# Mixture-of-experts layer on one core: order within expert pairs, per-expert release of the up matrices, order of the routing lists

## The reference, cut to what matters

```
idx, wts = route(h, w_router, e_bias)          # 8 of 64 experts for each of the 384 tokens
y = (silu(h @ ws1) * (h @ ws3)) @ ws2          # the shared expert, all tokens
  + sum over the 8 chosen experts e of  wts * ((silu(h @ w1[e]) * (h @ w3[e])) @ w2[e])
x = LN2(alpha * x + gate2 * y)
```

## Time and profile before

| | us |
|---|---|
| median of three runs | 1279.81 |
| the profiled execution, its own time | 1282.54 |
| its span, first to last instruction | 1280.4 |
| TensorE busy in it | 1021.1 (80%) |
| DMA packets of SP's queue, share of 16 engines' time | 65.9% |

### The profile page before, as it was taken

How to read it: one execution, slowest core, us unless ns; L and a number is a source line. 1 busy time by engine, 2 the same in 40 slices (tenths; PEclk the granted TensorE clock), 3 DMA queues, 4 the chain that set the end, 5 groups by cost and what they waited for, 6 DMA issues and landing times.

```text
span 1280.4 us, 23838 instructions
## 1 busy us (share of the span) xinstructions
PE 1021.1 (80%) x8392; PEld 652.9 (51%) x8393; DVE 432.4 (34%) x835; ACT 276.5 (22%) x515; POOL 220.1 (17%) x364
## 2 busy tenths in 40 slices
PE   4899999977676999985768888887777778776665
PEld 3898878756565444543335554444344334433332
DVE  4433343447742313876312112111111111112118
ACT  2322223325464000111112222111111111111100
POOL 0011100001300000202223323232222222223101
PEclk9899999988898999997889999999998899899888
DMA  9575535547266195085995698999999999999865
GB/s 348 180 254 196 181 125 183 177 167 258 79 235 211 63 345 175 33 346 164 317 333 212 245 346 298 384 383 394 385 385 384 376 370 374 379 383 382 348 243 214
DMA packets 97896, 347.52 MB, mean 271 GB/s; under 512 B 15041, under 2 KB 20209, under 8 KB 73130
## 3 DMA queue, kind: packets, MB, share of 16 engines
q1 hardware_dynamic: 81162, 311.56, 65.9%
q0 software_dynamic: 13936, 30.13, 7.2%
q10 hardware_dynamic: 2736, 4.98, 1.1%
HBM read 329.41 MB, written 29.52 MB: 280 GB/s over the span
## 4 chain that ended last, share of the span: by engine, by line
DMA 24%; PE 21%; issue 4%; DVE 2%; SPq 1%; ACT 1%; DVEq 0%; POOLq 0%; POOL 0%; ACTq 0%
DMA W<-w 22%; PE PS L1914 8%; PE PS L1899 6%; PE PS L1930 3%; PE PS L1968 2%; PE PS L1954 2%; DMA hT<-h_rows,tokens 1%; PE PS L1888 1%; DVE hido L2030 1%; SPq L1439 1%; ACT sgo L1997 1%; PE PS L1922 0%; DVE hidTo L2033 0%; SPq L1440 0%; DMA W<-expert_rows 0%
## 5 line engine op out<-in xcount | busy, mean ns | idle before, releaser
L1899 PE MATMUL PS<-W,XT 128*32 128x256 f32 x2048 | 141.1, 435 | 65.6 <-DMA W<-w 57.0
L1899 PEld LDWEIGHTS PS<-W,XT 128*32 128x32 f32 x2048 | 83.9, 125 | 136.9 <-issue 115.4
L1914 PE MATMUL PS<-W,XTo 128*64 128x256 f32 x1216 | 139.4, 381 | 0.0
L1914 PEld LDWEIGHTS PS<-W,XTo 128*64 128x64 f32 x1216 | 88.9, 137 | 41.3 <-issue 4.6
L303 PE MATMUL PS<-w_hi,u_hi 128*128 128x512 f32 x240 | 94.2, 392 | 1.5 <-DVE w_lo L427 1.0
L303 PE MATMUL PS<-w_hi,u_lo 128*128 128x512 f32 x240 | 93.5, 389 | 0.0
L303 PE MATMUL PS<-w_lo,u_hi 128*128 128x512 f32 x240 | 93.4, 389 | 0.0
L1954 PE MATMUL PS<-middle,hidT 128*32 128x512 f32 x512 | 66.7, 625 | 31.8 <-issue 30.5
L427 DVE TENSOR_TENSOR w_lo<-raw,w_hi 128x2048 fp32r<-128x2048 f32 x26 | 59.5, 2288 | 89.4 <-ACT w_hi L369 89.4
L1983 ACT ACTIVATE sg<-PS 64x256 f32<-64x256 f32 x32 | 12.1, 378 | 355.1 <-PE PS L1899 355.1
L1930 PE MATMUL PS<-middle,hidTo 128*64 128x512 f32 x304 | 73.6, 601 | 16.3 <-DVE hidTo L2033 16.3
(11 more groups left out here) (375 smaller groups left out, 1537.6 us busy)
## 6 DMA issues: line engine op xcount, KB each, us to landing
W<-w SPq DMA_DIRECT2D x128, 1024.0 KB, 14.1
middle<-w SPq DMA_DIRECT2D x64, 1024.0 KB, 16.9
raw<-w_in SPq DMA_DIRECT2D x26, 1024.0 KB, 5.3
wada<-w_ada SPq DMA_DIRECT2D x6, 2048.0 KB, 7.6
W<-expert_rows SPq DMA_DIRECT2D x16, 512.0 KB, 9.7
kc<-cache_k_diff SPq DMA_DIRECT2D x8, 512.0 KB, 5.0
vc<-cache_v_diff SPq DMA_DIRECT2D x8, 512.0 KB, 3.7
middle<-expert_rows SPq DMA_DIRECT2D x8, 512.0 KB, 15.4
```

What stands on the lines that cost most here:

```text
L1899: mm = pe.matmul(PS[64 * h + 32 * c:64 * h + 32 * c + 32, UP_B + i, 0:F], XT[:, i, k, 32 * c:32 * c + 32], t.W13[:, 2 * i + c, h, k], star ...
L1914: mm = pe.matmul(PS[64 * h:64 * h + 64, XH_B, 0:F], XTo[:, k], t.W13[:, slot, h, k], start=k == 0, stop=k == KD - 1)
```

## The change

Three edits. (1) In `rank_i` the two progressions swap places: of a pair the expert with few tokens now stands first, the one with many second. (2) SP asks for the up matrices of pair n+2 expert by expert: after the pair's `up` and the extra blocks of the first place, the first two matrices; after the extra blocks of the second place, the other two. `load_up` and `load_down` take one slot instead of a pair for that. (3) In the routing TensorE does the list products of tiles 0 and 1 ahead of `shared_down` of tile 2.

```diff
-            pool.iota(both[:, :, 0], pattern=[[1, (E - WB) // 2]], base=WB, channel_multiplier=0).then_inc(iota_done, 1)
-            pool.iota(both[:, :, 1], pattern=[[-1, (E - WB) // 2]], base=E - 1, channel_multiplier=0).then_inc(iota_done, 1)
+            pool.iota(both[:, :, 1], pattern=[[1, (E - WB) // 2]], base=WB, channel_multiplier=0).then_inc(iota_done, 1)
+            pool.iota(both[:, :, 0], pattern=[[-1, (E - WB) // 2]], base=E - 1, channel_multiplier=0).then_inc(iota_done, 1)
...
+def load_up(sp, t, slot, e):
+
+    sp.dma_start(t.W13[:, slot, 0], of_expert(t.w1v, e)).then_inc(t.wup_in[slot // 2], 16)
+    sp.dma_start(t.W13[:, slot, 1], of_expert(t.w3v, e)).then_inc(t.wup_in[slot // 2], 16)
...
             pe.wait_ge(ws2_in, 16)
-            for n in range(NT):
+            for n in range(NT - 1):
                 shared_down(n)
-            for n in range(NT):
+            for n in range(NT - 1):
                 lists(n)
+            shared_down(NT - 1)
+            lists(NT - 1)
...
                     sp.wait_ge(h_mm, n + 1)
-                    used = sp.value_load(t.ov[0:1, bass.ds(n * 2 + 2, 1)], min_val=0, max_val=XB)
-                    sp.wait_ge(o_h, used + 1)
-                    stand_alone(sp)
-                    load_up(sp, t, i, of_next)
+                    for c in range(2):
+                        used = sp.value_load(t.ov[0:1, bass.ds(n * 2 + (c + 1), 1)], min_val=0, max_val=XB)
+                        sp.wait_ge(o_h, used + 1)
+                        stand_alone(sp)
+                        load_up(sp, t, 2 * i + c, of_next[c])
                     sp.wait_ge(yy_mm, n + 1)
                     stand_alone(sp)
-                    load_down(sp, t, i, of_next)
+                    for c in range(2):
+                        load_down(sp, t, 2 * i + c, of_next[c])
```

More of the change, by code:

```diff
@@ L1433, in of_expert, with load_down @@
     return w[e] if isinstance(e, int) else w[bass.ds(e, 1)].rearrange("e p k n -> (e p) k n")
[L1436 to L1446, removed]
+def load_up(sp, t, slot, e):
+    sp.dma_start(t.W13[:, slot, 0], of_expert(t.w1v, e)).then_inc(t.wup_in[slot // 2], 16)
+    sp.dma_start(t.W13[:, slot, 1], of_expert(t.w3v, e)).then_inc(t.wup_in[slot // 2], 16)
+def load_down(sp, t, slot, e):
+    sp.dma_start(t.W2[:, slot], of_expert(t.w2v, e)).then_inc(t.wdown_in[slot // 2], 16)
 def fetch_rows(pool, t, dst, places, done):
@@ L1504, in _ @@
             for i in range(PW):
-                first = [E // WB * (2 * i + c) for c in range(2)]
-                load_up(sp, t, i, first)
-                load_down(sp, t, i, first)
+                for slot in (2 * i, 2 * i + 1):
+                    load_up(sp, t, slot, E // WB * slot)
+                for slot in (2 * i, 2 * i + 1):
+                    load_down(sp, t, slot, E // WB * slot)
         @block.tensor
```

## The result

The changed kernel took 1269.88 us (median of 9 runs), the kernel before 1277.86 beside it on the same chip: ratio 0.9929, 95% interval 0.9902 to 0.9957. By the ratio that is 9 us less (5.5 to 12.5), where I forecast 4.0. One of the nine executions took 5505 us; it counts in the median and not in the ratio. The profiled execution took 1265.68 us (span 1263.6).

A forecast was written before the change was run, and what follows sets the result against it. TensorE was taken to pace the kernel up to pair 11, the weight transfers afterwards. Head start -5.3, pair 0 +0.5 and routing +0.8 gave -4.0 us: from 1279.8 to 1275.8 us, forecast range 1273.5 to 1278.5.

The forecast's parts named there:

- The routing: Term for the reordered lists: tile 2's list ends later, delaying the expert stage by 0.8 us, or 1.6 with a wait.
- The head start: Expert stage: light half of pair 9's up matrices goes out 10.9 us earlier, so the weight stream ends 5.3 us sooner.
- stall by row traffic: Rival, pairs 3 to 7: extra blocks' gathers and scatters share engines with the light half; one 7 us stall, 1282.8, chance 0.12.
- binding releases: Rival, late pairs: the 27.53 us is latency, not queue; 5.3 us saved in some nine steps, 1232, chance 0.03.
- evened engines: Rival: the swap moves busy rows and extra blocks' rows to different DMA engines, 6 us more come free, 1270, chance 0.09.
- From 794.97 on it never is [empty]: Weight stream: from SP's request for pair 9's up matrices the DMA queue is never empty until the last pairs.
- only makes the queue longer: Saturated stretch, from 970 us on: engines are never free, so an earlier release there gains nothing.
- My term of +0.5 for pair 0: Pair 0: an early load beside a late gather may delay its rows; 0.5 us lost, between 0 and 5.4.

The follow-up runs named there:

- e5: Only the third part of the change (list products of tiles 0 and 1 ahead of tile 2's shared product), against the kernel before: ratio 1.0017 (0.9987 to 1.0047).
- e2: Only the swap of the places, up matrices still released together, lists as before, against the kernel before: ratio 0.9990 (0.9965 to 1.0016).
- e7: Places swapped, lists as before; light half early only from pair 10 on, both halves together in pairs 0 to 9; against the kernel before: 0.9964.
- e11: The whole change, unchanged, measured a second time, against the kernel before: ratio 0.9918 (0.9890 to 0.9947).
- e3: Early release of the light expert's half without the swap, lists as before, against the kernel before: ratio 0.9929 (0.9904 to 0.9953).
- e4: The change without its third part (swap and release expert by expert, lists as before), against the kernel before: ratio 0.9921 (0.9892 to 0.9949).
- e12: The change without its third part, measured again beside the whole change on one chip; against the kernel before: ratio 0.9914 (0.9882 to 0.9946).
- e8: The change without its third part, light half also waiting until DVE has formed the pair's hidden rows; against the kernel before: 0.9907 (0.9872 to 0.9942).
- e1: The kernel before, unchanged, run again for a second profile: 1286.1 us (one run).
- e6: Places swapped, lists as before; light half early only in pairs 0 to 9, both halves together from pair 10 on; against the kernel before: 0.9923.
- e9: Places swapped, lists as before; both halves asked for together, only when the pair's last extra block is copied out; against the kernel before: 1.0003.
- e10: Places swapped, lists as before; first place's half at the old time, second's when the last extra block is copied out; against the kernel before: 0.9982.
- e13: Places swapped, lists as before; from pair 10 on both halves only when the last extra block is copied out; against the kernel before: 0.9973.
- e14: Places swapped, lists as before; from pair 10 on up matrices asked for only with the down matrices, after the down product; against the kernel before: 0.9957.
- e15: Places swapped, light half early everywhere; from pair 10 on busy half only when the last extra block is copied out; against the kernel before: 0.9888.
- e16: Places swapped, light half early everywhere; from pair 10 on busy half only after the pair's down product; against the kernel before: 0.9893.

## Why the prediction was wrong

**What held.** The routing: forecast 0.8 us later, measured 0.70 (e5 and the change). The head start: forecast 5.3; pairs 3 to 12 took 198.5 us before and 194.1 after, 4.4 less. Every kernel that is early up to pair 9 has H 193.1 to 194.6, every one that is pairwise there 197.2 to 199.1. No stall by row traffic came up, and nothing like the 48 us of binding releases. The rival that gave a time near the result, 1270 by evened engines, was wrong in its mechanism: e2 has the swap and no gain. The Trainium skill, "DMA: Bandwidth & Descriptors", section "The descriptor swizzle", gives the formula by which I took the swap to change nothing. It gives it for a transfer to 128 partitions, and I assumed it for gathers of 64 rows; e2's 0.9990 agrees.

**What failed** is the step "From 794.97 on it never is [empty]", with the sentence that an earlier release there "only makes the queue longer". By it the pace of the saturated stretch stays as it is, and the sum has no term for it. e7 shows the contrary: its light half is early from pair 10 on alone, and S is 324.7 us, against 328.8 to 330.3 in the four kernels that are pairwise throughout; its whole time is 0.9964 (0.9939 to 0.9989) of before. I read the step from shares of 1.01 and 1.02 over 16 and 36 us. A finer view of the same trace speaks otherwise. Before, 1 us at a time, around SP's request of 991.42 to 992.85 us:

```profile
989.00:990.00 1.00, 1.00 (x13) 0.66 (x10) 0.00 (x0) 0.00 (x0) 0.98 (x2) 1.00 0.89 369
990.00:991.00 1.00, 1.00 (x12) 0.49 (x8) 0.00 (x0) 0.00 (x0) 0.00 (x0) 1.00 0.96 352
991.00:992.00 1.00, 0.80 (x10) 0.57 (x8) 0.38 (x1) 0.54 (x2) 0.00 (x0) 1.00 0.74 193
992.00:993.00 1.00, 0.30 (x2) 0.20 (x2) 0.51 (x2) 1.00 (x2) 0.00 (x0) 1.00 1.05 311
```

After the change, around the requests at 1011.82 and 1015.31:

```profile
1010.00:1011.00 1.00, 1.00 (x20) 0.51 (x13) 0.00 (x0) 0.05 (x1) 0.00 (x0) 1.00 1.02 426
1011.00:1012.00 1.00, 1.00 (x14) 0.79 (x13) 0.55 (x1) 0.84 (x2) 0.18 (x1) 1.00 1.04 434
1012.00:1013.00 1.00, 1.00 (x14) 0.64 (x11) 0.07 (x1) 0.07 (x1) 0.32 (x1) 1.00 1.03 418
1013.00:1014.00 1.00, 1.00 (x12) 0.66 (x10) 0.00 (x0) 0.00 (x0) 0.87 (x2) 1.00 0.96 377
1014.00:1015.00 1.00, 1.00 (x11) 0.45 (x7) 0.00 (x0) 0.00 (x0) 0.00 (x0) 1.00 1.01 401
```

Before, a quarter of the engines' time is missing in the microsecond in which the request goes out, and the bytes fall to half (the view counts a packet where it starts). Counted packet by packet, 16 are under way up to 989.2 us, 12 from 991.25 to 992.25, and 16 again from 992.75, when the new loads move. The Trainium skill, "Perfetto Trace Analysis", section "Identifying the Most-Contended Engine", calls the occupancy of 16 DMA engines misleading; the trace agrees, 0.74 in one microsecond inside a stretch (920 to 1000 us) that reads 1.01. The share of the 16 engines in the 4 us around each request, from 954 us on in both (after: the light halves), is

```
before  0.97 1.04 0.93 1.05 0.91 1.03 0.86 1.05 0.79 1.04 0.94
after   1.00 1.01 1.02 1.02 1.02 0.95 1.02 0.87 1.01 0.95 1.01
```

Every second request of before finds engines run dry, down to 0.79 at 1104 us. After the change it begins later and is weaker (0.95, 0.87 and 0.95 at 1049, 1086 and 1121 us). It is so in the other profiles: counted as packets under way, the first such request from pair 8 on is that of pair 16 in all four pairwise kernels, and that of pair 19 to 22 in the seven with the change's releases in the stretch (after, e11, e3, e4, e12, e8, e7). A load is counted in 16 parts, and they don't land in step: the last 16 counts of U(31) come between 1207.1 and 1215.3 us, and its last two loads were full 9 us apart. I had that row, but drew nothing from it for the releases. Where 12 packets are under way ahead of a request and 16 behind it, some engines had nothing to do until SP asked again, however much the others still held.

How much is it? I counted the weight packets of the traces (8 KB each, 128 a matrix, 768 a pair). The lead is what had been moved when a pair's up product starts beyond what that pair needs (up matrices to its own, down matrices of earlier pairs), in matrices. The rate, the mean length and the share of time with fewer than 16 packets of any kind under way are those of S:

```
                      pair 0-3    H      S   lead at 12, 30  packets/us  ns   under 16
before                   69.2   198.5  330.3   1.9   3.4        42.5     339    6.1%
e1, before again         69.3   199.1  329.1   1.7   3.3        42.6     338    6.0%
e2, swap alone           69.3   198.2  328.8   1.8   3.2        42.6     340    4.9%
e5, lists alone          70.2   198.4  328.8   1.6   3.3        42.7     338    4.9%
after                    65.6   194.1  324.4   1.9   3.7        43.3     335    2.3%
e11, after again         68.0   193.4  324.5   2.0   3.6        43.2     336    2.3%
e3, early, no swap       69.1   194.6  323.1   2.1   3.6        43.4     334    3.1%
e4, lists as before      67.3   194.0  324.5   1.9   3.5        43.2     335    2.9%
e12, the same            69.3   193.2  324.8   1.8   3.7        43.3     335    2.4%
e8, light 0.4 later      67.0   193.9  324.4   1.6   3.3        43.3     335    2.5%
e6, early to 9           66.5   194.1  326.8   2.1   3.1        42.7     338    4.6%
e7, early from 10        71.0   197.8  324.7   1.4   3.7        43.5     335    2.2%
e9, late                 68.9   204.2  327.0   1.8   2.0        42.4     337    7.9%
e10, late split          68.4   197.7  328.9   1.5   3.2        42.7     338    5.1%
e13, late from 10        70.2   197.2  325.5   1.4   1.9        42.7     337    7.0%
e14, later from 10       69.2   197.8  324.7   1.6   1.7        42.6     336    6.8%
e15, busy half late      69.0   193.1  322.9   1.8   3.0        43.3     335    2.8%
e16, busy half later     67.7   193.9  325.5   1.7   3.2        43.0     335    4.9%
```

S is (18 x 768 + 128 x growth of the lead) / rate. That holds by the way the terms are counted and is no cause, but it parts S in two. *The rate:* with an early half from pair 10 on it is 43.0 to 43.5 in nine profiles, without it 42.4 to 42.7 in nine others. 1.5% of 329 us is 4.9 us, the missing gain. It comes about where the pairwise requests begin to find engines dry: from pair 12 to 18 the seven early kernels take 109.2 to 111.8 us and the four pairwise ones 110.0 to 111.3, from pair 18 to 30 they take 212.6 to 214.9 against 217.5 to 220.1. *The lead:* with pairwise requests 1.4 to 1.7 matrices more are moved ahead of need by pair 30; 1.5 are 192 packets, 4.5 us of all engines' work. With late requests (e9, e13, e14) it grows by 0.1 to 0.5 only, and S is 2.3 to 4.5 us shorter than the pairwise mean of 329.3, without any gain in rate. So asking earlier inside a saturated stretch isn't neutral, as I took it to be, nor is it good in itself: an early light half goes with a higher rate, a late request with a smaller lead. Whether the two add is open: with the busy half put off S is 322.9 in e15 and 325.5 in e16, against 324.4 for the change.

Summed for the change, against the pairwise kernels: routing +0.7; pairs 0 to 3, mean of the two profiles 66.8 against 69.5, -2.7; H -4.8; S -4.8; and pair 31 gives back some 1.1 us (16.3 us from pair 30 to 31, against 14.8 to 16.2). In all -10.5, beside the measured 9 and 10.5. The sum forecast +0.8, +0.5, -5.3 and nothing for these stages: the saturated stretch is the term that was left out, and pairs 0 to 3 came out the other way, for which no run gives the cause. The forecast's range of 1273.5 to 1278.5 doesn't follow from the bounds of its terms either, which add to 1274.2 at best (-5.5, 0, +0.8, -0.9) and 1282.8 at worst (-4.9, +5.4, +1.6, +0.9).

**What stays open.** *Why the rate is higher.* The rate is the weight packets under way divided by their length. From the four pairwise kernels to the seven with the change's releases the first goes from 14.43 to 14.51 (0.6% more) and the second from 338.7 to 334.8 ns (1.2% less). So engines kept from running dry are about a third of the gain in rate, and shorter packets two thirds. Of the weight packets that start in the 2 us after a pairwise request 15 to 17% take over 420 ns, after an early light half 0 to 2%; in all of S it is 11 to 12% and 10%. That may be engines that start from standstill; but the pairwise request also falls into the microseconds in which gathered rows arrive, when packets are long in every kernel (below), and the two aren't told apart. And e13 and e14 run dry still more often (7%) at an unchanged rate, with packets of 336 to 337 ns, while e16 with 4.9% has a rate of 43.0, so dry time alone isn't the measure. No trace names the engine that moved a packet. *Why moving ahead costs the others time:* that engines share something is the plain reading, but only argued. *Pairs 0 to 3:* the kernels that are early there take 65.6 to 69.3 us, the pairwise ones 69.2 to 71.0. Part of it is pair 1's 1.6 us, which is there in all early kernels but e15 and which no row explains. The rest may be the granted clock, which from 600 to 668 us changes between 2.4 and 1.2 GHz (a mean of 0.83 to 0.90 over the 18 profiles): pair 0's up product alone took 5.2 to 6.3 us, where 3.66 is usual. My term of +0.5 for pair 0 doesn't show: its wait for rows was 0.6 to 2.3 us in the early kernels and 0.8 to 2.4 in the pairwise ones.

## What to carry to other kernels

A mean busy share of 1.00 over several transfers doesn't say that an earlier request is worthless: look at it microsecond by microsecond around each request, and at the time between the last two counts of one load, before costing a deeper queue at nothing. Then ask for whom the earlier transfer is: here the half that was asked for early in the saturated stretch was worth 4.6 us there (e7), while asking late for what nobody yet needed was worth nearly as much (3.8 and 4.5 us, e13 and e14). And split a forecast into head start and pace, since a release that is moved in every pass of a loop acts on both. Last, read from the trace of an experiment whether its edit moved what it was to move: e8's wait looked like half of the lead and took off a tenth.

## What was unexpected of the hardware

The share of DMA time goes above 1 because packets overlap: from 900 to 1160 us of before, 17 packets were under way on the 16 engines for 19% of the time and 18 for 3%. So a share of 1.01 doesn't tell whether the engines are full: it is read from 803 to 819 us, where there were never fewer than 16 packets, and from 920 to 1000 us, where there were fewer for 5% of the time.

A weight packet takes 314 ns as a rule, but 394 to 508 ns (means of single microseconds) from 991 to 997 us of before, where rows of 4 KB arrive. POOL had issued a gather at 988.79 and one at 994.23, and no scatter until 997.07, so these are gathered rows; beside the row packets from 1002 to 1005, behind scatters of 997.07 and 999.78, weight packets take 310 to 316. It is so in all 18 profiles: in the stretch from 2.5 to 0.5 us ahead of a gather's landing weight packets take 384 to 456 ns, ahead of a scatter's 310 to 315.

And asking 4.7 to 6.9 us later for the next up matrices, with some engine dry for 7% of the time, made the kernel 3.5 to 5.5 us faster (e13, e14).
